# Up projection of a ConvFFN by seven block products instead of eight from the fourth pair on, with the split of the feed-forward operand moved into the down projection

## The reference

```
def conv_ffn(h, conv_state, w_ffn_up, conv_w, conv_b, w_ffn_down):
    u = h @ w_ffn_up                                   # (544, 1024) @ (1024, 5632)
    ext = jnp.concatenate([conv_state, u], axis=1)
    c = conv_b + sum(conv_w[i] * ext[:, i:i + T] for i in range(3))
    g, val = c[..., :2816], c[..., 2816:]
    f = (gelu(g) * val) @ w_ffn_down                   # (544, 2816) @ (2816, 1024)
    return f, ext[:, -2:]
```

## Time and profile before

| What | us |
|---|---|
| median of 3 runs | 1011.24 |
| lowest and highest of them | 1010.37, 1011.36 |
| span of the profiled execution, first to last instruction | 1007.0 |
| busy in it: PE, weight load, VectorE, ScalarE, GpSimd | 984.8, 876.5, 552.8, 378.3, 177.8 |
| DMA, mean over the span | 174 GB/s |

### The profile page before, as it was taken

One profiled execution on the slowest core, in us unless ns is written; L12 is line 12 of the kernel. 1 busy time (PEld: TensorE's weight loads), 2 busy tenths in 40 slices (PEclk: granted clock), 3 DMA queues, 4 the chain that ended last, 5 costly groups with the idle time before them and its releaser, 6 DMA issues.

```text
span 1007.0 us, 20394 instructions
## 1 busy us (share of the span) xinstructions
PE 984.8 (98%) x7774; PEld 876.5 (87%) x7774; DVE 552.8 (55%) x912; ACT 378.3 (38%) x832; POOL 177.8 (18%) x365
## 2 busy tenths in 40 slices
PE   5999999999999999999999999999999999999997
PEld 4788787779999899999887789999999999777775
DVE  5355125435377778784146777666666666422225
ACT  6233222441543333333133654444444444212413
POOL 2102004044152343436100001000000000000100
PEclk9999999999999999999999999999999999999999
DMA  6734445546796676669635424555545553221323
GB/s 242 258 138 162 167 174 168 191 155 199 255 308 216 202 235 209 213 207 315 210 104 172 126 77 168 179 177 174 176 166 177 172 193 123 85 84 64 121 84 118
DMA packets 40465, 175.36 MB, mean 174 GB/s; under 512 B 6936, under 2 KB 7384, under 8 KB 38864
## 3 DMA queue, kind: packets, MB, share of 16 engines
q1 hardware_dynamic: 25616, 125.78, 36.2%
q0 software_dynamic: 14784, 48.65, 15.4%
HBM read 164.40 MB, written 54.05 MB: 217 GB/s over the span
## 4 chain that ended last, share of the span: by engine, by line
PE 91%; DVE 3%; ACT 2%; DMA 2%; issue 1%; POOL 0%; SPq 0%; DVEq 0%; ACTq 0%
PE bank L1339 11%; PE bank L1340 10%; PE bank L1341 10%; PE bank L1860 9%; PE bank L1861 9%; PE bank L1859 9%; PE bank L1421 6%; PE bank L1427 6%; PE bank L1426 6%; PE bank L1358 3%; PE bank L1321 2%; PE bank L1756 1%; PE bank L1762 1%; PE bank L1761 1%; PE bank L1616 1%
## 5 line engine op out<-in xcount | busy, mean ns | idle before, releaser
L1950 DVE TENSOR_TENSOR wlo<-wraw,whi 128x1024 fp32r<-128x1024 f32 x88 | 107.5, 1222 | 274.0 <-ACT whi L839 273.7
L839 ACT ACTIVATE whi<-wraw 128x1024 fp32r<-128x1024 f32 x90 | 95.3, 1059 | 316.8 <-PE bank L1341 203.2
L1860 PE MATMUL bank<-T1l,whi 128*128 128x288 f32 (+1 forms) x704 | 203.7, 289 | 0.0
L1861 PE MATMUL bank<-T1h,wlo 128*128 128x288 f32 (+1 forms) x704 | 203.3, 289 | 0.0
L1859 PE MATMUL bank<-T1h,whi 128*128 128x288 f32 (+1 forms) x704 | 202.6, 288 | 0.2 <-DVE wlo L2414 0.2
L1859 PEld LDWEIGHTS bank<-T1h,whi 128*128 128x128 f32 x704 | 133.2, 189 | 0.4 <-DVE wlo L2414 0.4
L1860 PEld LDWEIGHTS bank<-T1l,whi 128*128 128x128 f32 x704 | 132.8, 189 | 0.0
L1861 PEld LDWEIGHTS bank<-T1h,wlo 128*128 128x128 f32 x704 | 132.3, 188 | 0.0
L1339 PE MATMUL bank<-whi,T1h 128*128 128x512 f32 (+1 forms) x288 | 114.0, 396 | 0.5 <-POOL wlo L613 0.3
L1421 PE MATMUL bank<-T1h,whi 128*128 128x272 f32 x384 | 113.5, 295 | 0.0
L1427 PE MATMUL bank<-T1h,wlo 128*128 128x272 f32 x384 | 111.1, 289 | 0.0
(11 more groups left out here) (302 smaller groups left out, 1816.6 us busy)
## 6 DMA issues: line engine op xcount, KB each, us to landing
wraw<-in_weights SPq DMA_DIRECT2D x142, 512.0 KB, 3.7
out_s_kv_g<-in_cache_kv_g SPq DMA_DIRECT2D x64, 511.0 KB
qbc<-sample_queries POOLq DMA_DIRECT2D x48, 256.0 KB, 5.1
kvk<-in_cache_kv_g POOLq DMA_DIRECT2D x32, 256.0 KB, 4.5
kvv<-in_cache_kv_g POOLq DMA_DIRECT2D x16, 512.0 KB, 7.9
out_s_kv_g<-in_cache_kv_g SPq DMA_DIRECT2D x16, 508.0 KB
S<-in_state_ret POOLq DMA_DIRECT2D x16, 256.0 KB, 3.3
out_s_ret<-S POOLq DMA_DIRECT2D x16, 256.0 KB, 6.3
```

Source lines behind the costliest of these rows:

```text
L839: nc.scalar.activation(w_halves(s)[0], wraw[:, s % 2, :], ACT.Copy).then_inc(w_hi, 1)
L1860: mm(dst, Wh, T1l[:, k, c], start=False, stop=False)
L1861: last = mm(dst, Wl, T1h[:, k, c], start=False, stop=k == KT - 1)
L1950: v.tensor_tensor(lo, wraw[:, s % 2, :], hi.bitcast(F), ALU.subtract).then_inc(w_lo, 1)
```

## The change

The first three pairs stay as they are, but with the halves cut at 256 and 288 columns and without HEAD_COLS, and the whole stage is written out instead of looped. From pair n = 3 on, a pair is seen as a product of 2 x 2 blocks: gate and value tile, lower and upper half of K (4 tiles each), first and second half of the tokens (272 columns each). Strassen's way, in the form with shared sums, needs seven block products instead of eight. Six of them are made in three passes (12 instructions); product 4, whose weights are the value tile's upper half, is made by four plain float32 instructions on an operand that is not split.

The products accumulate in a row in one bank where the results share them: 1, 6, 7 and 4 in bank_a (ScalarE copies the bank out after 1, 6 and 7: `keep_first`, `keep_second`, `keep_third`), 5 and 3 in bank_c, 2 in bank 6. VectorE adds these to make the gate tile (`gate_first`, `gate_second`) and part of the value tile (`value_second`); the rest is ScalarE's `value_first`.

The four sums of token blocks (t1 to t4) are made once from the whole hidden rows (`whole_operand`), beside pairs one and two. The sums of weight blocks are made for each pair: SP loads the value tile's lower half twice side by side (`load_v_low`), and GpSimd adds to it, by one accumulating DMA from DRAM, the gate's lower and the value's upper half (`add_to_v_low`); VectorE makes two more sums (`sum_2`, `sum_4`). The gate slot and both sum tiles are split by ScalarE and VectorE as the slots are now, three tiles for a pair instead of two. There are two sets of these buffers, and set 1 lies on the slots' buffers and their split parts, so that pair 4's sums wait for pair 2 to end.

The first tap of the convolution goes from VectorE to ScalarE (an Identity with scale and bias). f is kept unsplit, and split in the down projection: f 0 to 3 in the last pair, then two f for each slot. It has no room otherwise, so x after the mixer goes to DRAM before the up projection and comes back for the last sum. Some semaphores are merged to make room for new ones.

```diff
-HEAD_COLS = {0: slice(0, 128), 1: slice(128, 256), 4: slice(256, 288), 2: slice(288, 416), 3: slice(416, 544)}
-UP_HALVES = ((0, 288), (288, 256))
+UP_HALVES = ((0, 256), (256, 288))
+NPLAIN = 3
+NSKIP = 2 * (FT - NPLAIN)
...
+def up_products():
+    order = [(NPLAIN, 1), (NPLAIN, 2)]
+    for n in range(NPLAIN, FT):
+        nxt = n + 1 < FT
+        order += [(n, 6), (n, 5), (n, 7)] + [(n + 1, 1)] * nxt + [(n, 4), (n, 3)] + [(n + 1, 2)] * nxt
+    return order
+PRODUCTS = up_products()
+PRODUCT_NO = {key: k + 1 for k, key in enumerate(PRODUCTS)}
...
+        def load_v_low(n):
+            src = w_dram[S_UP + 2 * n + 1][:, 512:SLOT].unsqueeze(1).broadcast_to([128, 2, 512])
+            sp.dma_start(s13_raw[pair_set(n)][:].rearrange("p (a c) -> p a c", a=2), src).then_inc(vl_in[pair_set(n)], 16)
+        def load_v_high(n):
+            sp.dma_start(v_high[pair_set(n)][:], w_dram[S_UP + 2 * n + 1][:, 0:512]).then_inc(vh_in[pair_set(n)], 16)
+        for s in range(S_UP + 2, S_UP + 2 * NPLAIN):
+            load_one(s)
+            move(*next(moves))
+        sp.wait_ge(w_used, S_UP)
+        load_v_low(NPLAIN)
+        load_g(NPLAIN)
+        load_v_high(NPLAIN)
+        load_v_high(NPLAIN + 1)
+        sp.wait_ge(w_lo, S_UP + 2 * NPLAIN)
+        load_g(NPLAIN + 1)
+        sp.wait_ge(w_used, S_UP + 2 * NPLAIN)
+        load_v_low(NPLAIN + 1)
+        for n in range(NPLAIN, FT - 2):
+            sp.wait_ge(product, PRODUCT_NO[n, 2])
+            sp.wait_ge(s24_made, 2 * pair_no(n))
+            load_g(n + 2)
+            sp.wait_ge(product, PRODUCT_NO[n, 7])
+            load_v_low(n + 2)
+            move(*next(moves))
+            sp.wait_ge(product, PRODUCT_NO[n, 4])
+            load_v_high(n + 2)
...
+        def add_to_v_low(n):
+            e = pair_set(n)
+            pool.wait_ge(vl_in[e], set_count(n))
+            src = w_dram[S_UP + 2 * n:S_UP + 2 * n + 2].rearrange("s p (h c) -> p h s c", h=2)[:, 0]
+            pool.dma_start(s13_raw[e][:].rearrange("p (a c) -> p a c", a=2), src, accum_op=ALU.add).then_inc(sum_in[e], 16)
+        for n in range(3):
+            conv_heads(n)
+        add_to_v_low(NPLAIN)
+        for n in range(FT):
+            if n >= 1 and n + 2 < FT:
+                conv_heads(n + 2)
+            if n == NPLAIN - 1:
+                add_to_v_low(NPLAIN + 1)
+            if NPLAIN <= n < FT - 2:
+                add_to_v_low(n + 2)
...
+        def first_tap(n, j):
+            tile = n + FT * j
+            act.wait_ge(u_one[j], n + 1)
+            act.wait_ge(u_two[j], n + 1)
+            act.wait_ge(head_ready, conv_no(n, j))
+            if n >= 2:
+                act.wait_ge(f_done, n - 1)
+            nc.scalar.activation(cbs[:, n % 2, j, :], ubs[:, n % 3, j, 2:UW], ACT.Identity, scale=convp[:, tile, 2:3],
+                                 bias=convp[:, tile, 3:4]).then_inc(tap_one, 1)
...
+        def sums_13_hi(n):
+            e = pair_set(n)
+            act.wait_ge(sum_in[e], set_count(n))
+            if n >= NPLAIN + 2:
+                act.wait_ge(product, PRODUCT_NO[n - 2, 7])
+            elif e:
+                act.wait_ge(w_used, S_UP + 2 * NPLAIN)
+            nc.scalar.activation(s13_high[e][:], s13_raw[e][:], ACT.Copy).then_inc(s13_hi, 1)
...
+        def keep_third(n):
+            act.wait_ge(product, PRODUCT_NO[n, 7])
+            act.wait_ge(u_two[1], n)
+            nc.scalar.activation(rr[:], P[bank_a(n)][:, 0:HALF], ACT.Copy, scale=-1.0).then_inc(r_neg, 1)
...
+        for n in range(NPLAIN, FT):
+            first_tap(n - 1, 0)
+            keep_second(n)
+            if n + 1 < FT:
+                sums_13_hi(n + 1)
+            else:
+                act.wait_ge(product, PRODUCT_NO[FT - 2, 7])
+                act.sem_inc(w_hi, NSKIP)
+                w_split(S_DN)
+                w_split(S_DN + 1)
+            keep_third(n)
+            gelu(n - 1)
+            if n + 2 < FT and n > NPLAIN:
+                gate_hi(n + 2)
+            elif n == NPLAIN:
+                gate_hi(5)
+            if n + 1 < FT:
+                keep_first(n + 1)
+                sums_24_hi(n + 1)
+            else:
+                for k in range(4):
+                    f_high(k)
+            value_first(n)
+            first_tap(n, 1)
+        first_tap(FT - 1, 0)
+        gelu(FT - 1)
...
+        def three_passes(b, fresh, Wh, Wl, w0, Th, Tl):
+            for k in range(4):
+                cut = slice(w0 + 128 * k, w0 + 128 * k + 128)
+                mm(b[:, 0:HALF], Wh[:, cut], Th(k), start=fresh and k == 0, stop=False, skip_group_check=not fresh)
+                mm(b[:, 0:HALF], Wh[:, cut], Tl(k), start=False, stop=False, skip_group_check=not fresh)
+                last = mm(b[:, 0:HALF], Wl[:, cut], Th(k), start=False, stop=k == 3, skip_group_check=not fresh)
+            last.then_inc(product, 1)
...
+        def product_4(n):
+            e = pair_set(n)
+            pe.wait_ge(vh_in[e], set_count(n))
+            pe.wait_ge(t_raw, 6)
+            pe.wait_ge(r_neg, pair_no(n))
+            for k in range(4):
+                last = mm(P[bank_a(n)][:, 0:HALF], v_high[e][:, 128 * k:128 * k + 128], t4raw[:, k, :], start=False, stop=k == 3, skip_group_check=True)
+            last.then_inc(product, 1)
...
+        product_1(NPLAIN)
+        product_2(NPLAIN)
+        for n in range(NPLAIN, FT):
+            product_6(n)
+            product_5(n)
+            product_7(n)
+            if n + 1 < FT:
+                product_1(n + 1)
+            product_4(n)
+            product_3(n)
+            if n + 1 < FT:
+                product_2(n + 1)
+        pe.wait_ge(product, len(PRODUCTS))
+        pe.sem_inc(w_used, NSKIP)
...
+        def sum_2(n):
+            e = pair_set(n)
+            dve.wait_ge(sum_in[e], set_count(n))
+            dve.wait_ge(vh_in[e], set_count(n))
+            if n >= NPLAIN + 2:
+                dve.wait_ge(product, PRODUCT_NO[n - 2, 3])
+            elif e:
+                dve.wait_ge(w_used, S_UP + 2 * NPLAIN)
+            v.tensor_tensor(s24_raw[e][:, 0:512], s13_raw[e][:, 0:512], v_high[e][:], ALU.add).then_inc(s24_made, 1)
+        def sum_4(n):
+            e = pair_set(n)
+            dve.wait_ge(s24_made, 2 * pair_no(n) - 1)
+            dve.wait_ge(g_in[e], set_count(n))
+            v.tensor_tensor(s24_raw[e][:, 512:SLOT], s24_raw[e][:, 0:512], g_raw[e][:, 512:SLOT], ALU.add).then_inc(s24_made, 1)
+        def sums_13_lo(n):
+            e = pair_set(n)
+            dve.wait_ge(s13_hi, pair_no(n))
+            dve.wait_ge(s24_made, 2 * pair_no(n) - 1)
+            v.tensor_tensor(s13_low[e][:], s13_raw[e][:], s13_high[e][:].bitcast(F), ALU.subtract).then_inc(s13_lo, 1)
+        def sums_24_lo(n):
+            e = pair_set(n)
+            dve.wait_ge(s24_hi, pair_no(n))
+            v.tensor_tensor(s24_low[e][:], s24_raw[e][:], s24_high[e][:].bitcast(F), ALU.subtract).then_inc(s24_lo, 1)
...
+        whole_operand(0)
+        whole_operand(1)
+        w_split(S_UP + 2)
+        operand_3()
+        operand_1()
+        w_split(S_UP + 3)
...
+        for n in range(NPLAIN, FT):
+            if n > NPLAIN:
+                gate_second(n - 1)
+            gate_first(n)
+            conv(n - 1)
+            if n + 1 < FT:
+                sum_2(n + 1)
+                sums_13_lo(n + 1)
+            else:
+                dve.wait_ge(w_hi, S_DN + 1)
+                dve.sem_inc(w_lo, NSKIP)
+                w_split(S_DN)
+            value_second(n)
+            if n + 1 < FT:
+                sum_4(n + 1)
+            f_product(n - 1)
+            if n + 2 < FT:
+                gate_lo(n + 2)
+            if n + 1 < FT:
+                sums_24_lo(n + 1)
+            else:
+                w_split(S_DN + 1)
+                for k in range(4):
+                    f_low(k)
+        gate_second(FT - 1)
+        conv(FT - 1)
+        f_product(FT - 1)
...
         for s in range(2 * n):
+            for k in range(2 * s + 4, min(2 * s + 6, FT)):
+                f_low(k)
             if first + s + 2 < NSLOT:
                 w_split(first + s + 2)
...
```

More of the change, by code:

```diff
@@ new lines, in _ @@
+        act.wait_ge(convp_in, 16)
+        columns(0, 0)
+        w_split(S_UP + 2)
+        columns(0, 1)
+        w_split(S_UP + 3)
+        first_tap(0, 1)
+        first_tap(0, 0)
+        operand_hi(1, t3raw, t3hi)
+        operand_hi(2, t1raw, t1hi)
+        columns(1, 0)
+        w_split(S_UP + 4)
+        operand_hi(3, t2raw, t2hi)
+        gelu(0)
+        columns(1, 1)
+        w_split(S_UP + 5)
+        gate_hi(3)
+        sums_13_hi(3)
+        first_tap(1, 1)
+        first_tap(1, 0)
@@ new lines, in _ @@
+        columns(2, 0)
+        sums_24_hi(3)
+        gelu(1)
+        columns(2, 1)
+        first_tap(2, 1)
+        gate_hi(4)
+        keep_first(3)
+        for n in range(NPLAIN, FT):
[4 more added lines that the diff above has]
+            else:
+                act.wait_ge(product, PRODUCT_NO[FT - 2, 7])
```

(49 more changed lines are left out.)

445 lines of the change are left out of this document (303 added, 142 removed).

## The result

| What | before | after |
|---|---|---|
| median of the runs, us | 1010.81 (4 runs) | 1035.24 (4 runs) |
| lowest and highest, us | 1008.49, 1011.36 | 1029.78, 1037.42 |
| span of the profiled execution, us | 1007.0 | 1032.9 |

The ratio is 1.0244, with a 95% interval of 1.0225 to 1.0263: the changed kernel is 2.4% **slower**. The forecast was 997, in a range of 990 to 1014. The profiled execution took 1034.72, 1.8 above its span.

What follows compares the result with a forecast made beforehand. TensorE, busy 98% of the span, was taken as the bound. Saving 21.3 us, losing 0.8, 3.1 and 2.6 once, and 1 of slips, takes 1007.0 to 993; 4.2 for the runs' median gives 997, range 990 to 1014.

Steps and rivals of the forecast that it cites:

- L2: Up projection: time from GpSimd's issue of the accumulating DMA to its landing, taken as 6.5 to 7 us, bounds 4.4 and 15.8.
- L1: Up projection: time from SP's issue of load_v_low to its landing, for which GpSimd waits; taken as 3.5 us.
- just hidden: Up projection loop: with L2 of 7, L1 + L2 is 10.5 us, the most that TensorE's work covers.
- the rule: Up projection: where the DMA chain sets the loop, a pair's period is 5.7 + (L1 + L2)/2 us.
- The point at which the change turns slower: Up projection: losses exceed savings from a period of 11.65 us, L1 + L2 of 11.9, L2 of 8.4.
- the rival that the accumulation is the bound: Up projection: sums_13_hi and sum_2 wait for the accumulated tile; with L2 10, 16.5 us slower, 1028; chance 0.20.
- An undisturbed turn: Up projection, TensorE: a pair takes 10.97 us against 12.09, product 4 being 1.9 of it; 21.3 saved over 19 pairs.
- The loop of ScalarE and VectorE: Up projection: both engines' work fits in TensorE's 10.97 us a pair, VectorE with 0.7 to 1.3 to spare.
- Head: Start of the up projection: whole_operand ahead of w_split(S_UP + 2) on VectorE makes TensorE go on 0.8 us later.
- First turn: Start of the new pairs: load_v_low(4) waits for plain pair 2 to end, a late landing costing 3.1 us once.
- Down projection: Its start: P4 waits 0.6 us and the first f splits delay sample_part(1), 2.6 lost in all; later splits hidden.
- ScalarE's tables: Rival, up projection: first_tap's Identity forces table loads, 2.6 us more ScalarE a pair, total 1001 to 1008; chance 0.03.

Runs made afterwards that it cites:

- run 3: The changed kernel with its accumulating DMA made plain (sums left out) and the window copies moved from the loop to the down projection; 1000.69 us, one execution.
- Run 9: run 6's kernel with ScalarE's copies columns(2, 1) and keep_first(3) put ahead of gelu(1), before the loop; 995.77 us, ratio 0.9866.
- run 6: The changed kernel with GpSimd adding the weight sums instead of the accumulating DMA, and waiting for the previous pair's sums_24_lo; 997.26 us, ratio 0.9875.
- runs 5: The changed kernel with the accumulating DMA replaced by plain loads from SP and a sum on GpSimd; 1001.04 us, ratio 0.9906.
- run 8: run 6's kernel with window copies moved to the down projection and w_split(S_UP + 2) put between the two whole_operand halves; 1001.83 us, ratio 0.9916.

## Why the prediction was wrong

**The step that failed** is the price of the accumulating DMA: "I take 6.5 to 7, near the middle plus something for the second read", of L2, and "L1: a weight slot of 512 KB lands 3.5 after its issue". They measured 8.5 and 5.26: of the 3.3 by which L1 + L2 is over the 10.5 that was "just hidden", 1.8 are L1's and 1.5 L2's. The shares are not sharp: the 3.5 was a time to landing, where the medians are now 4.8 for L1 and 7.2 for L2, and the 8.5 is the mean of the 12 late tiles. By the rule 13.8 is a turn of 12.6, 19 x (12.6 - 10.97) = 31 us of the 38 by which the forecast missed. The other 7 are as much as 19 times the 0.4 between the rule and the measured 12.99, for which the prediction had no term; the stretches at half clock, 10 us at most, are large enough for it. The mechanism and the rule were right, as the table shows. The point at which the change turns slower was put at 11.9, and the rival that the accumulation is the bound, with L2 10 and 1028 at 0.20, is what happened, though with a smaller L2 and a larger L1. L2 had bounds and a rival; L1, with half of the error, had neither. Its row was read in a stage at a DMA share of 0.49, while the prediction's own working put the share at 77 to 90% after: a duration from the less loaded stage was carried into a more loaded one. The whole stage after the change has 0.70, and the long turn above 0.82 to 0.87. The work of the engines was priced well: 0.70 of 12.99 is 9.1 us a pair, inside its 8.4 to 9.9; what was not priced is that transfers take longer to land under it. Nor is all of L1's error load: in run 3, without the moves and the add, the same transfer still lands after 4.0, and its rows are 2 KB where a slot's are 4 KB. What of that 0.5 is due to the rows no run tells. For L2 the 7.9 of GpSimd's loads in rows of 1 KB was the better guide.

**The 3.2 of the Trainium skill.** The Trainium skill (DMA: Bandwidth & Descriptors, Anatomy of one DMA) gives a GpSimd-issued DMA about 2.0 us and its bytes over 436 GB/s, an estimate of 3.2 for 512 KB. The traces do not agree: 4.7 to landing, plain and without moves beside it, and 7.2 with the add and the moves. It was right to go by the rows, which were still too low.

**TensorE, right.** An undisturbed turn was put at 10.97 and is 10.9. Product 4 was put at 1.9 with the switch. In an undisturbed turn (not shown) it begins at 847.33 and the second product behind it at 849.29; less one step of 0.124, that is 1.84.

**The loop of ScalarE and VectorE, right.** With the landings of run 3 the order fits into TensorE's turn without a gap, and what a late landing holds was named: `sums_13_hi` with `keep_third` and product 4 behind it. The loop from the tile's arrival to the next P7 was put at 11.4; it is 11.13 in the turn shown and 12.74 in the loop before it, where a stretch at half clock falls into it. That stretch was not in the prediction.

**Head, right.** TensorE goes on at 608.93 and not at 606.57; less the lead of 1.67 that was there at 510 us, 0.7 against the 0.8 put down.

**First turn, wrong in its cause.** 3.1 were put on `load_v_low(4)`; its accumulated tile is only 0.2 late. What TensorE waits for is another thing. The timelines of VectorE, ScalarE and TensorE there:

```profile
626.82 0.69 DVE L2853 TENSOR_TENSOR s_raw<-s_raw,v_high 128x512 f32<-128x512 f32 x1 [6.03 <-DMA s_raw<-in_weights]
```

```profile
637.94 0.67 ACT L1444 ACTIVATE c<-c 128x560 f32<-128x560 f32 x1 [6.40 <-DVE c L2780]
...
640.09 1.04 ACT L1459 ACTIVATE g_high<-g_raw 128x1024 fp32r<-128x1024 f32 x1
641.03 0.37 ACT L1486 ACTIVATE s<-bank 128x272 f32<-128x272 f32 x1
```

```profile
628.70 0.39 PE L2143 MATMUL bank<-T1h,whi 128*128 128x256 f32 x1 [1.41 <-DVE wlo L2309]
...
641.55 0.51 PE L2189 MATMUL bank<-t2hi,s_high 128*128 128x272 f32 x1 [3.52 <-ACT s L1486]
```

`keep_first(3)` stands on ScalarE behind gelu(1), which waits 6.40 for VectorE's convolution of pair one, and VectorE makes that only after all the sums and splits of pair 3, ahead of which it waits 6.03 for the accumulated tile of pair 3. The prediction summed VectorE's 27 us against 33 of TensorE, "hidden". It did not ask what VectorE itself waits for in between, nor what is queued on ScalarE behind an instruction that waits for their end. The 1.41 at 628.70 have the same source: the split that TensorE waits for there stands behind that tile. That the size, 3.5, is near the 3.1 is luck. The lateness that was forecast is there too, but lies under this wait: without it product 6 would have begun at 638.03, and the tile of pair 4 is read at 645.20, 7.2 later, against the 7.6 of the prediction. Run 9 shows the place of `keep_first` to be a cause, in the kernel of run 6. That VectorE's 6.03 is another is not shown by a run of its own; where the tile comes earlier, in runs 5 and 6, VectorE waits 2.91 and 3.23 for it, and product 6 waits 2.10 and 2.44.

**Down projection, right.** P4 waits 0.58 and the sample parts 0.32 and 0.83, 1.7 in all, where 2.6 were put down. The split of f beside the down projection costs nothing: 145.1 us against 145.2 from its first prompt product on. Nor does reloading the residual rows, which is in the same 145.1.

**ScalarE's tables, right.** There is no table load for the Identity of `first_tap`. But it takes 0.86, and not the 0.68 of the earlier trace rows at which it was priced:

```profile
L1438 ACT ACTIVATE c<-u,convp 128x560 f32<-128x560 f32 x44 | 37.4, 856 | 20.3 <-DVE u L2888 19.6
```

That TensorE's saving can be had was right too: run 6 comes to 997.26 with another way to make the sums, though with a turn of 11.1 set by VectorE. Left open is how much the clock takes of the longer turns; 10 us is the most.

## What to carry to other kernels

A DMA latency on a loop's path has to be priced at the load of the changed stage, not at that of the stage in which its row was read; and where a first part of it is hidden, two causes that each look free may together be over the edge, so compare the sum with the edge and give each term a range. A DMA that adds to its destination is to be priced above a plain one of the same bytes, and where GpSimd is free an add there may be better (run 6), if its place is chosen so that VectorE's next urgent instruction is not beside it. Before a wait is taken out of a filled head, look at who is queued behind the next one on the other engines: of two such edits here, run 9 moved most of a wait to the next engine, and run 8 made a longer one.

## What was not expected of the hardware

- **An add in the DMA** of 512 KB in rows of 2 KB lands 1.1 us later than the plain write, without the moves (medians 4.7 and 5.8) and beside them (6.1 and 7.2). Over the turns in which ScalarE waited, L2 differs by 1.4 and by 2.15. What of it is the adding and what the read of the destination no run tells.
- **GpSimd and VectorE hold each other off.** A VectorE instruction with two SBUF inputs grows from 1.22 to 3.38, and two taps from 1.51 to 3.18, beside a GpSimd sum that takes 2.39 to 3.41 itself.
- **Short stretches at half clock.** TensorE falls to 1.2 GHz for some 3.4 us, when or soon after it goes on behind a gap of 2 to 4 us, in seven of nine such gaps here, while the clock line on the profile's page still shows 9 in each slice: the windows and the spacing of the products are where it is seen.
